# Two transformer blocks on one core: the indexer ahead of the differential keys, and norms by row tile

## The reference

```python
for l in range(2):                                  # block two
    h = rms_norm_2(x, attn_norm_g[l]); proj = h @ w_in[l]
    (mq, mk, mv, dq, dk, dv, sq, sk, sv, iq, ik, iw) = split(proj)
    moba = moba_attention(...)                      # 4 heads, causal
    lam = exp(sum(lp[0]*lp[1])) - exp(sum(lp[2]*lp[3])) + lam_init
    diff = (softmax(q1 k1) - lam * softmax(q2 k2)) v        # 4 heads, causal
    diff = rms_norm_2(diff, diff_subln_g[l]) * (1 - lam_init)
    # dsa: the indexer chooses the top 64 causal keys of each query
    score = sum_h iw * relu(iq_h . ik);  sel = top_k(score, 64)
    dsa = softmax(q k[sel]) v[sel]                  # 4 heads
    x = x + concat(moba, diff, dsa) @ w_out[l]
    h2 = rms_norm_2(x, ffn_norm_g[l])
    x = x + (silu(h2 @ w_gate[l]) * (h2 @ w_up[l])) @ w_down[l]
```

## Time and profile before

| | us |
|---|---|
| median of three runs | 1726.59 |
| lowest, highest | 1725.46, 1727.4 |
| the profiled execution | 1726.47 |
| its span | 1724.7 |
| mean granted clock of TensorE, of full speed | 0.976 |

### The profile page before, as it was taken

How to read it: one execution, slowest core, us unless ns; L and a number is a source line. 1 busy time by engine, 2 the same in 40 slices (tenths; PEclk the granted TensorE clock), 3 DMA queues, 4 the chain that set the end, 5 groups by cost and what they waited for, 6 DMA issues and landing times.

```text
span 1724.7 us, 23563 instructions
## 1 busy us (share of the span) xinstructions
PE 1613.1 (94%) x9246; PEld 1319.9 (77%) x9246; DVE 1049.5 (61%) x1599; ACT 768.5 (45%) x1288; POOL 118.4 (7%) x130
## 2 busy tenths in 40 slices
PE   6999899999999989989999998689999997699999
PEld 3865686788888877578988776579998775589997
DVE  4537654753465356666765656658884657568873
ACT  3435523641354224545654455334454564345442
POOL 1010000100000001000000211000000101000000
PEclk9999999999999999999999999799999999799999
DMA  9349333873377324749997785136656684146653
GB/s 360 116 149 314 109 92 117 294 250 98 120 264 252 97 73 147 255 145 304 310 312 225 221 271 195 50 111 183 184 185 192 199 267 159 50 135 183 184 185 119
DMA packets 201005, 322.42 MB, mean 187 GB/s; under 512 B 14576, under 2 KB 100864, under 8 KB 200768
## 3 DMA queue, kind: packets, MB, share of 16 engines
q1 hardware_dynamic: 192992, 293.51, 53.2%
q0 software_dynamic: 7680, 27.34, 4.4%
q10 hardware_dynamic: 224, 0.07, 0.0%
HBM read 298.27 MB, written 22.61 MB: 186 GB/s over the span
## 4 chain that ended last, share of the span: by engine, by line
PE 82%; DVE 10%; issue 2%; DMA 2%; ACT 2%; POOL 1%; SPq 0%; POOLq 0%; DVEq 0%; ACTq 0%
PE bank L1833 50%; PE pair_bank L1833 20%; PE bank L1893 2%; PE pair_bank L2074 1%; PE bank L2102 1%; PE pair_bank L2120 1%; DMA raw<-in_w_in 1%; DVE w_lo L1339 1%; PE bank L2085 1%; DVE wide L1423 1%; PE bank L2134 1%; PE bank L2310 1%; PE bank L2015 1%; POOL xrstd L910 1%; DMA raw<-in_w_ada 1%
## 5 line engine op out<-in xcount | busy, mean ns | idle before, releaser
L1339 DVE TENSOR_TENSOR w_lo<-raw,w_hi 128x1024 fp32r<-128x1024 f32 (+1 forms) x374 | 448.6, 1220 | 307.9 <-ACT w_hi L1031 305.5
L1031 ACT CAST w_hi<-raw 128x1024 fp32r<-128x1024 f32 (+2 forms) x416 | 428.1, 1043 | 408.0 <-PE bank L1833 304.6
L1833 PE MATMUL pair_bank<-act_hi,w_hi 128*128 128x256 f32 (+1 forms) x736 | 232.9, 316 | 11.9 <-DVE act_lo L1413 5.6
L1833 PE MATMUL pair_bank<-act_hi,w_lo 128*128 128x256 f32 (+1 forms) x736 | 229.3, 311 | 0.0
L1833 PE MATMUL pair_bank<-act_lo,w_hi 128*128 128x256 f32 (+1 forms) x736 | 229.1, 311 | 0.0
L1833 PE MATMUL bank<-w_hi,hid_lo 128*128 128x512 f32 x560 | 221.7, 396 | 0.0
L1833 PE MATMUL bank<-w_hi,hid_hi 128*128 128x512 f32 x560 | 221.6, 396 | 0.0
L1833 PE MATMUL bank<-w_lo,hid_hi 128*128 128x512 f32 x560 | 221.6, 396 | 0.0
L1833 PE MATMUL bank<-w_hi,act_hi 128*128 128x512 f32 (+2 forms) x528 | 211.5, 400 | 4.5 <-DVE act_lo L1413 2.6
L1833 PE MATMUL bank<-w_lo,act_hi 128*128 128x512 f32 (+2 forms) x528 | 204.0, 386 | 0.0
L1833 PE MATMUL bank<-w_hi,act_lo 128*128 128x512 f32 (+2 forms) x528 | 203.3, 385 | 0.0
(11 more groups left out here) (228 smaller groups left out, 2142.6 us busy)
## 6 DMA issues: line engine op xcount, KB each, us to landing
raw<-in_w_mlp SPq DMA_DIRECT2D x128, 512.0 KB, 4.5
raw<-in_w_in SPq DMA_DIRECT2D x112, 512.0 KB, 4.0
raw<-in_w_ada SPq DMA_DIRECT2D x96, 512.0 KB, 5.4
raw<-in_w_gate SPq DMA_DIRECT2D x44, 512.0 KB, 3.7
raw<-in_w_up SPq DMA_DIRECT2D x44, 512.0 KB, 3.8
raw<-in_w_down SPq DMA_DIRECT2D x44, 512.0 KB, 3.6
split_lo<-w_lo POOLq DMA_DIRECT2D x36, 512.0 KB, 4.8
w_lo<-split_lo SPq DMA_DIRECT2D x36, 512.0 KB, 4.7
```

The lines of the kernel that those rows point to most:

```text
L1031: nc.scalar.copy(hi_of(i)[:, 0:w], raw[:, i % RAW, 0:w]).then_inc(hi_ready, 1)
L1339: nc.vector.tensor_tensor(w_lo[:, i % RAW, 0:w], raw[:, i % RAW, 0:w], hi_of(i)[:, 0:w].bitcast(F32), ALU.subtract).then_inc(lo_ready, 1)
L1833: ins = nc.tensor.matmul(o, a[x], b[y], start=first and i == 0, stop=True, skip_group_check=True)
```

## The change

It has three parts.

1. **Block two's tables.** The blocks of rows2 are now dq, iq, mv_ik, dk, mqk, sqk, dv, sv, and the units are numbered accordingly. The logits stand behind slots 12 to 17, the search of row tile 0 behind 14 to 20, and `score 0` behind slot 18 instead of 11. From there one attention step follows each slot, two at 27. `search 1` lies between slots 22 and 28. In `out2`, the steps 12 to 15 and mixes 0 to 7 are placed anew, `turn_rows` ahead of `weigh 14`.
2. **Norms by row tile.** In the last slots of mlp1 of layer 1, out2, and mlp2 of layer 0 (`TAIL`: 4 or 2 slots) PE does row tile 2 over all of these slots, then row tile 3. DVE, ACT and GpSimd norm tile 2 meanwhile. Rows2's first block goes through its four slots for tile 2 and again for tile 3, whose transposes stand ahead of the fourth slot. There the 28 filler transposes are gone; for m = 5 and 7 they stand between the two tiles' transposes.
3. **Opening.** Slot 0 of rows1 (now the 13th load) goes between `ada 3` and `ada 1`, slot 1 behind `ada 1`; the first norm goes in quarters.

```diff
-        BLOCKS2 = (("dq", DQ), ("dk", DK), ("iq", IQ), ("mv_ik", IK), ("mqk", MQ), ("sqk", SQ), ("dv", DV), ("sv", SV))
+        BLOCKS2 = (("dq", DQ), ("iq", IQ), ("mv_ik", IK), ("dk", DK), ("mqk", MQ), ("sqk", SQ), ("dv", DV), ("sv", SV))
...
-            22: [("drain", 5, 0), ("turn", 8), ("drain", 5, 1), ("score", 8), ("gather", 5), ("search", 0, 3)],
+            22: [("drain", 5, 0), ("weigh", 3), ("drain", 5, 1), ("score", 4), ("second", 8), ("search", 1, 1)],
+            23: [("turn", 8), ("weigh", 4), ("score", 5), ("first", 9)],
...
+        AHEAD1 = {0: 2, 1: 0}
...
+        TAIL = {4: 4, 5: 2, 6: 4, 7: 2}
+        def xn_of(m):
+            return xn_beside if m == 6 else xn2
...
         class Scalar(Splitting):
+            def tail(self, key, l, h, slots, m):
+                halves = sorted({ch for ch, _ in slots})
+                self.step()
+                for ch in halves:
+                    self.square(m, 2, ch, (key, l, h, ch, 2))
+                for _ in slots[1:]:
+                    self.step()
+                if m % 2 == 0:
+                    for a in range(2):
+                        self.norm_high(m, 0, a)
+                for ch in halves:
+                    self.square(m, 3, ch, (key, l, h, ch, 3))
...
         class Vector(Splitting):
+            def tail(self, key, l, h, slots, m):
+                halves = sorted({ch for ch, _ in slots})
+                self.step()
+                for ch in halves:
+                    self.add(key, l, h, ch, 2, (2, 3))
+                self.stats(m, 2)
+                if m % 2:
...
+                    self.stats(m, 3)
+                    self.norm_row(m, 2)
+                    self.norm_row(m, 3)
...
+                else:
+                    self.step()
+                    self.norm_row(m, 2)
+                    for ch in halves:
+                        self.add(key, l, h, ch, 3, (2, 3))
+                    for a in range(2):
+                        self.norm_low(m, 0, a)
+                    self.stats(m, 3)
+                    self.step()
+                    self.norm_row(m, 3)
+                    self.step()
+                    for a in range(2):
+                        self.norm_low(m, 1, a)
...
         class Tensor(Phases):
             def norm2(self, m, l, which):
-                self.keep_busy()
...
+                self.turn_row(m, 0)
+                if m % 2:
+                    self.keep_busy()
+                    self.turn_row(m, 1)
...
             def rows2(self, l):
+                first = self.i
+                for t in range(TT):
+                    for q in range(4):
+                        if t == 0:
+                            if q == 3:
+                                self.turn_row(m, 1)
+                            self.split_done(first + q)
```

More of the change, by code:

```diff
@@ L354, in build @@
-            27: [("mix", 11), ("turn", 10), ("score", 12), ("search", 1, 3)],
-            28: [("mix", 0), ("mix", 1), ("mix", 2), ("mix", 3), ("drain", 7, 0), ("weigh", 12), ("drain", 7, 1), ("score", 13),
-                 ("square", 0), ("search", 1, 2)],
+            8: [("first", 2), ("second", 2)],
+            9: [("turn", 2), ("first", 3), ("second", 3)],
+            10: [("turn", 3), ("drain", 2, 0), ("drain", 2, 1)],
+            11: [("first", 4), ("second", 4), ("index_scale",)],
@@ L358, in build @@
         OUT2 = {
[L359 to L361 removed]
+            0: [("mix", 0), ("mix", 1), ("mix", 2), ("mix", 3), ("weigh", 12), ("square", 0), ("score", 13), ("mix", 4), ("mix", 5), ("mix", 6),
+                ("mix", 7), ("square", 1)],
+            1: [("norm", 0), ("weigh", 13), ("score", 14), ("norm", 1)],
```

334 lines of the change are left out of this document (201 added, 133 removed).

## The result

| | before | changed |
|---|---|---|
| median, us | 1726.99 (4 runs) | 1744.91 (4 runs) |
| lowest to highest | 1725.46 to 1728.4 | 1740.08 to 1747.71 |
| ratio, 95% interval | | 1.0099 (1.0083 to 1.0116) |
| profiled execution: time, span | 1726.47, 1724.7 | 1747.71, 1745.9 |
| mean granted clock | 0.976 | 0.969 |

The change costs 17.9 us. The forecast was slower by 8.9 us, and 1735.5 us; the measured time lies at the top end of the range given. The direction held, the size was half of what was measured. Note that the changed kernel's runs spread over 7.6 us, before's over 2.9, and that the profiled execution is the slowest of the four, 2.8 us above the median.

What follows compares the result with a forecast made beforehand. TensorE, with 82% of the chain of waits, was taken to bound the kernel, through its idle time or clock. Terms 4.4 + 4.8 + 4.7 - 13.5 - 1 + 10 = +9.4 on 1726.47 gave 1735.9, stated as 1735.5; range 1717 to 1745.

Steps and rivals of the forecast that it cites:

- The tables: Block two's new order: each stage takes 177.1 us against 172.7 and 172.3, so +4.4 and +4.8.
- steps 0 to 12: Block two's attention steps, each lasting DVE's list between two maxima plus 1.1 to 1.7 us turn-around; 68.2 us in all.
- step 7: Block two's attention step with a unit's first half and a split on DVE; predicted to take 7.2 us.
- step 4: Block two's attention step: 4.9 us by DVE's list, 2.2 longer because ACT's squares for unit 10 delay its exponentials.
- The clock: Both layers' block two: new gaps on PE lower its clock, +5 us per layer, +10 in all.
- Layer 0's wait: Start of rows2 in layer 0: parameters, tables and lambdas make the first turn late, +4.7 us, bounds 0 and 6.3.
- the rival of starved parameters: Layer 0's eight GpSimd parameter loads, held by DVE's instructions, end up to 5 us later; 1740 us, chance 0.05.
- Norms: Row-tile norms: -6.3 and -5.4 ahead of rows2, +0.35 twice ahead of up2; -13.5 with low-clock savings.
- Opening: Start of the kernel: slot 12's matmuls fill PE's early gaps, -1 us, bounds 0 and -2.5.
- The clock kept up: Rival: gaps of 2 to 3.3 us don't lower PE's clock, so +10 goes; 1725.5 us, chance 0.19.
- the faster case: Rival: block two's steps go at PE's pace of 4.6 us; 1699.5, or 1717.5 with half of it; chance 0.18.
- The clock low through the whole chain: Rival: low clock over steps 1 to 12 costs +12 us per layer instead of +5; 1749.5 us, chance 0.12.

Runs made afterwards that it cites:

- e4: Changed kernel with filler transposes of a constant on PE in its waits for the probabilities of steps 1, 3 to 7 and 9 to 11; 1740.3 us.
- e7: Changed kernel with unit 8's second half moved ahead of the weighing of step 3; 1745.3 us.
- e1: Kernel before with only the change's block two tables (order of blocks and units, FILL2, OUT2); 1753.6 us.
- e9: Changed kernel with GpSimd loading the later norms' gain rows behind rows2's slot 9 instead of right behind the norm; 1743.3 us.
- e8: Changed kernel with the old tables, the old norms for m = 5 and 7, and dq's drains one slot earlier; 1720.0 us.
- e12: Changed kernel with old tables, old norms m = 5, 7, gain rows late, drains early, lambdas late, and fillers at steps 11, 12, 13, 15; 1705.9 us.
- e2: Changed kernel with the old blocks, units, FILL2 and OUT2 put back, norms by row tile and opening kept; 1725.5 us.

## Why the prediction was right and wrong

**The tables: right.** The rule that a step takes DVE's list plus the turn-around gave 68.2 for steps 0 to 12; with the clock held, both layers have 68.3. That the sum meets it to 0.1 is in part luck: 0.7 of e4's 68.3 is the late filler of step 7, and the other steps together are 0.6 below their lists. The extra 2.2 us of step 4 by ACT's square were there (7.1), and e7 took them away. That the new order gives back in waits what it saves before step 12 is what e1 measured: +26 us for the tables alone. Here the prediction had only +9.2 before the clock, plus the clock's 10.

**The clock: right mechanism, mis-sized term.** This is the step that made the forecast too small. +10 was put in for both layers. By the table, the sums of the prediction (177.1 for each stage, and 4.7 for the wait) are exceeded by 12.7 us in layer 0 and 8.1 in layer 1, 20.8 in all. Of this the clock is: 2.7 behind the wait at the start of layer 0, 3.8 and 2.5 in steps 0 to 12, and in steps 12 to 15 and the end some 4.7 and 2.3 (29.1 and 26.8 for the 25.3 and 25.2 of e4, 19.8 and 19.6 for the 18.9 of the prediction): 16. With step 7, whose list was right at 7.2 and which took 7.8, it is some 17. The term was sized from the matmul time lost in two stretches of before, without working out how many stretches the listed gaps would start: eight in layer 0 and five in layer 1, each with some 1.7 us of matmul time or more. The other 3 to 4 us are small errors of the lists: 0.4 and 2.4 up to the first score and 0.9 per layer in steps 12 to 15, less 0.6 per layer in steps 0 to 12.

The profiled execution came out 21.2 us longer in span where +9.4 was forecast. The missing 11.8 are some 7 of the clock, 3 to 4 of the lists, 2.8 of the norms for m = 5 and 7 and the 1.0 counted twice, less the 2.7 of block one. This execution is the slowest of the four. How much of the 17.9 between the medians is clock is therefore known only roughly: e4's fillers got 4.6 of it back by the medians, and 12.0 between the two profiles, of which the changed kernel's is its slowest execution and e4's its fastest.

**Layer 0's wait: right size by the wrong mechanism.** 4.7 was predicted, 4.80 measured. The step that failed here is "ACT's lambda instruction ... stands ahead of the dq drains" as the cause. It does stand there, but behind it stood a cast whose load was late. The prediction put the wait at the first turn; it was at iq's second product. The low clock behind it (2.7) had no place in the sum. The parameter issues on GpSimd took 0.54 to 0.80 us each after the change too, as in the earlier trace rows, and e9, which leaves them where they are, more than halved the wait; so the rival of starved parameters fell. The Trainium skill (SBUF — State Buffer, section "SBUF: two separate sides") says that a transfer issued by GpSimd can wait for a VectorE operation that locks the port the two share; no issue at this place shows a wait of that kind.

**Norms: right for m = 4 and 6, short for m = 5 and 7.** -6.3 and -5.4 came as worked out (-6.3, -5.5). For the odd ones +0.35 was predicted (9.4 for 9.05, without a sum) and +1.8 and +1.7 measured. The filler and the transposes took 3.2 and 1.1 us before; they now stand behind a wait of 3.1 that has no filler, with the clock low, and take 4.0 and 2.0. The -1.5 in up2 and mlp2 came too, but e8 and e12, with the old norm there, have the same 188.1, so it needs no new norm.

**Opening: right in sign, its size not settled.** -1.0 was predicted and shows in this profile. With the same opening, the stretch to the last rows1 matmul took 103.6 to 106.1 us in the profiles of e2 to e12, and 106.8 in e1, which has the old one. The other 2.7 us in block one were in no term, and they are luck of the one execution: with the same code there, the profiles of e2 to e12 have 855.1 to 859.6 for the changed kernel's 855.6.

**Rivals.** The clock kept up and the faster case fell. The clock low through the whole chain fell as a mechanism, since the granted clock over steps 0 to 12 was 0.86 and 0.90 and came back to 1.00 between the stretches; but its 1749.5 is nearer to the measured 1744.9 than the forecast's 1735.5, since the low stretches cost some 17 rather than the 10 of the forecast or its own 24.

## What to carry to other kernels

Where a chain of small steps runs over several engines, add up the list of the engine in the middle between two of its fixed points, with one measured turn-around: it gave 68.2 for 68.3. Then count the gaps that this leaves on TensorE and price each as a stretch of matmul time at half clock; a filler of constant transposes in the gap removes that price where it ends before the wait does (4.6 us in one kernel, 7.4 in another, by the medians); where the slot ahead of it ran at the low clock, a filler of 2.78 us ended behind the wait and cost 0.7. And when a stage starts earlier, list what is issued at its start on every DMA queue: a ring slot that is kept for two passes and two 512 KB rows loaded beside it turned a gain of 6.3 us into a wait of 4.8, and three things in a row had to be moved before it went.
